# Moving a gated linear recurrent unit in front of the attention, with its input projections as seven-product tiles

## The reference, cut to what matters

```python
proj = h @ w_in                      # 1024 x 9216
q, k, v, g_att, u, g_lru, merge = jnp.split(proj, split_at, axis=-1)
y_a = (dilated_attention(q, k, v) * silu(g_att)) @ w_pa
u = causal_depthwise_conv(u, conv_w, conv_b)          # 4 taps
y_b = (rg_lru(u, ...) * silu(g_lru)) @ w_pb
gate_a, gate_b = jnp.split(sigmoid(merge), 2, axis=-1)
out = (gate_a * y_a + gate_b * y_b) @ w_o
```

## Time and profile before

| | |
|---|---|
| median of the timed runs | 2789.05 us |
| the profiled execution, its own time | 2786.48 us |
| its span | 2784.7 us |
| PE busy | 98% of the span |
| DVE, ACT, POOL busy | 72%, 56%, 11% |
| sets, from the first product to the last | 1753.67 to 2096.39 us |
| attention, up to the first tile of the recurrent unit | 2096.39 to 2344.88 us |

### The profile page before, as it was taken

One profiled execution on the slowest core, in us unless ns is written; L12 is line 12 of the kernel. 1 busy time (PEld: TensorE's weight loads), 2 busy tenths in 40 slices (PEclk: granted clock), 3 DMA queues, 4 the chain that ended last, 5 costly groups with the idle time before them and its releaser, 6 DMA issues.

```text
span 2784.7 us, 33128 instructions
## 1 busy us (share of the span) xinstructions
PE 2733.2 (98%) x13148; PEld 2280.7 (82%) x13148; DVE 2000.1 (72%) x2300; ACT 1558.0 (56%) x1724; POOL 301.9 (11%) x179
## 2 busy tenths in 40 slices
PE   8999999969999999999999998999999999999999
PEld 7888788858888888888888887888888888888887
DVE  7554457778888888888888888755555565666664
ACT  5322322247777777777777776322335666997122
POOL 0211000020000000000000001332321111112000
PEclk9999999989999999999999999999999999999999
DMA  6222248689999999999999964243333443114442
GB/s 198 95 75 65 87 153 291 247 344 375 385 385 386 387 386 386 386 384 390 384 386 384 386 228 164 95 121 111 101 121 134 129 122 102 49 48 144 169 149 91
DMA packets 181546, 628.30 MB, mean 226 GB/s; under 512 B 43920, under 2 KB 78096, under 8 KB 125840
## 3 DMA queue, kind: packets, MB, share of 16 engines
q1 hardware_dynamic: 176496, 609.46, 58.8%
q0 software_dynamic: 4464, 16.25, 2.2%
q10 hardware_dynamic: 432, 0.47, 0.1%
HBM read 557.74 MB, written 67.21 MB: 224 GB/s over the span
## 4 chain that ended last, share of the span: by engine, by line
PE 95%; DVE 3%; ACT 1%; DMA 1%; issue 0%; SPq 0%; DVEq 0%; ACTq 0%
PE bank L468 25%; PE bank L470 25%; PE bank L469 25%; PE bank L1894 13%; PE bank L476 3%; PE bank L2801 1%; PE bank L485 1%; PE bank L1443 1%; PE bank L794 1%; PE bank L3299 0%; DVE r_sc L1677 0%; DVE r_at L1678 0%; DVE r_best L1674 0%; PE bank L2802 0%; PE bank L854 0%
## 5 line engine op out<-in xcount | busy, mean ns | idle before, releaser
L1842 DVE TENSOR_TENSOR e_wl<-e_raw,e_wh 128x2048 fp32r<-128x2048 f32 x381 | 870.8, 2291 | 123.9 <-ACT e_wh L1834 123.5
L1834 ACT ACTIVATE e_wh<-e_raw 128x2048 fp32r<-128x2048 f32 x384 | 735.7, 1919 | 184.4 <-PE bank L470 101.0
L468 PE MATMUL bank<-e_wh,e_xh 128*128 128x512 f32 x1020 | 403.4, 395 | 0.0
L470 PE MATMUL bank<-e_wh,e_xl 128*128 128x512 f32 x1020 | 398.1, 390 | 0.0
L469 PE MATMUL bank<-e_wl,e_xh 128*128 128x512 f32 x1020 | 396.9, 389 | 0.0
L470 PEld LDWEIGHTS bank<-e_wh,e_xl 128*128 128x128 f32 x1020 | 191.4, 188 | 41.0
L469 PEld LDWEIGHTS bank<-e_wl,e_xh 128*128 128x128 f32 x1020 | 191.8, 188 | 38.1
L468 PEld LDWEIGHTS bank<-e_wh,e_xh 128*128 128x128 f32 x1020 | 191.6, 188 | 38.0 <-DVE e_wl L1842 0.4
L1894 PE MATMUL bank<-e_wh,e_hh 128*128 128x512 f32 x512 | 159.1, 392 | 0.0
L1894 PE MATMUL bank<-e_wl,e_hh 128*128 128x512 f32 x512 | 157.8, 389 | 0.0
L1894 PE MATMUL bank<-e_wh,e_hl 128*128 128x512 f32 x512 | 157.8, 389 | 0.0
(11 more groups left out here) (579 smaller groups left out, 5864.3 us busy)
## 6 DMA issues: line engine op xcount, KB each, us to landing
e_raw<-in_e_gate_dram SPq DMA_DIRECT2D x128, 1024.0 KB, 7.2
e_raw<-in_e_up_dram SPq DMA_DIRECT2D x128, 1024.0 KB, 7.5
e_raw<-in_e_down_dram SPq DMA_DIRECT2D x128, 1024.0 KB, 7.7
b_raw<-in_w_sets_dram SPq DMA_DIRECT2D x18, 1024.0 KB, 5.3
a_raw<-in_w_dram SPq DMA_DIRECT2D x12, 1024.0 KB, 5.7
a_mod_w<-in_w_mod_dram SPq DMA_DIRECT2D x48, 256.0 KB, 4.7
b_raw<-in_w_dram SPq DMA_DIRECT2D x11, 1024.0 KB, 4.9
a_x<-in_x_dram SPq DMA_DIRECT2D x16, 512.0 KB, 4.5
```

What stands on the lines that cost most here:

```text
L468: e.matmul(out, a[0], b[0], start=first, stop=False)
L470: return e.matmul(out, a[1], b[0], start=False, stop=last)
L1834: e.activation(t.e_wh[s][:, 0:2048], t.e_raw[slot][:, 0:2048], ACT.Copy).then_inc(*e.inc("e_round", i))
L1842: e.tensor_tensor(t.e_wl[s][:, 0:2048], t.e_raw[slot][:, 0:2048], t.e_wh[s][:, 0:2048].bitcast(F32), ALU.subtract).then_inc(*e.inc("e_spli ...
```

## The change

The recurrent unit is computed beside the sets. All 8 of its tiles become sets, at the front of the list; one merge tile takes the place of one of them in the half tiles of the attention, and 25 sets of seven products replace 18. The set loop calls one step of the unit after each product: the block of channels ct uses the products 9 + 21 ct and on, and `step` is the number of products since. The results of a set of the unit are stored to DRAM, and loaded again for the convolution and for the Silu. The place of `l_u`, `l_cv` is won by shortening the ring to 6 and AHEAD to 4, and one of the crossed blocks is put over a quarter of the input `h`, which is stored before and loaded again at the end of the sets. The unit's result goes to DRAM and comes back after the attention. The computation of `decay` (34 small DVE instructions) moves from the start of the attention to the first layer. POOL, which made the rests of the unit's rounded input and of its gates' weights before, still makes them, and takes over the last product (with Silu of the gate) from DVE.

```diff
-N_SETS = 18
+N_SETS = 25
-AHEAD = 6
-UNIT_TILE, MERGE_TILE = 1, 9
+AHEAD = 4
+N_RING = 6
+MERGE_TILE = 2
-HALF_SLOT = (3, 0, 1, 2, 3, 0, 1, 2, 3, 0, 1, 3, 0, 1)
+HALF_SLOT = (1, 3, 2, 0, 1, 3, 2, 0, 1, 3, 2, 1, 3, 2)
+SET_KINDS = ([("lru", i) for i in range(8)] + [("values", 2 + i) for i in range(4)]
+             + [("qk", 4 + i) for i in range(8)] + [("merge", i) for i in range(5)])
+LRU_FROM, LRU_EVERY, LRU_GATES = 9, 21, 6
+def lru_step(q):
+    ct, k = divmod(q - LRU_FROM, LRU_EVERY)
+    return (ct, k) if 0 <= ct < 8 else (-1, 0)
 def set_bank(g, i):
-    return (7 * g + i) % 8
+    q = 7 * g + i
+    return (q + 4 * gates_ahead(q)) % 8
 (pe_set, after product q)
+        if lru_step(q)[1] == LRU_GATES:
+            pe_lru_gates(e, t, lru_step(q)[0])
 (the loops of ACT and DVE over q; DVE's has dve_lru_step, SP's sp_lru_step)
         act_set(e, t, *divmod(q, 7))
+        act_lru_step(e, t, *lru_step(q))
+    e.wait_ge(*e.at("lru_made", 7))
 (act_lru_step: step 0 Identity for the first tap; 3 the two Copies that round;
  8 and 9 four Sigmoids each; 10 Exp, Tanh, Square; 12 Sqrt, Silu)
+    if step == 12:
+        e.wait_ge(*e.at("lru_q", ct))
+        e.activation(tt[:, :], tt[:, :], ACT.Sqrt, scale=-1.0, bias=t.k["tiny"])...
+        e.wait_ge(*e.at("l_gl_in", ct))
+        e.activation(t.l_u[:, :], t.l_u[:, :], ACT.Silu)...
 (dve_lru_step: step 0 two taps, 1 the third; 11 the two products; 13 product and scan)
 (pool_second)
     for g in range(1, N_SETS):
         pool_set_sums(e, t, g)
+        ct = (g - 2) // 3
+        if g % 3 == 2:
+            pool_lru_step(e, t, ct, 4)
+        if g % 3 == 1 and g > 1:
+            pool_lru_step(e, t, (g - 4) // 3, 14)
+    pool_lru_step(e, t, 7, 14)
 (sp_lru_step: step 2 loads the gate's input, 10 the next gates' weights, 15 stores
  the result when lru_made and loads the next block's u)
 (sp_second)
+    e.wait_ge(*e.at("b_hid", 1, 3))
+    for part in range(2):
+        e.dma_start(t.scr_b21[part], t.b_hid[part][:, 0:4, 512:1024].bitcast(F32))...
+            if q == 7 * (N_SETS - 1) + 3:
+                e.wait_ge(*e.at("part_spent", q))
+                (both parts of the quarter are loaded again)
 (dve_low_crossed and act_round_crossed: crossed block 2 waits until the early tiles are done)
+    if n == 2:
+        e.wait_ge(*e.at("w_spent", 1))
+        e.wait_ge(*e.at("hid_out1"))
 (dve_lru)
+    dve_low_w(e, t, MERGE_TILE)
     attention_over(e)
```

More of the change, by code:

```diff
@@ L1221, in dve_first @@
             dve_s5_inputs(e, t, b)
+        if slot == 12:
+            dve_decay(e, t)
         if slot % 8 == 6:
@@ L2127, in last_part_of @@
 def last_part_of(h):
-    return max(q for q in range(N_PARTS) if q % 8 // 2 == h)
+    return max(q for q in range(N_PARTS) if q % N_RING // 2 == h)
 def tile_slot(i):
-    return i if i < N_EARLY else (i - UNIT_TILE) % 2
+    return i % 2
 def sp_load_w(e, t, i):
@@ L2817, in unit @@
             which, half = u[1:]
-            pe_channels(e, t, unit_bank(u), wt, whole, t.b_hid, half, 8, ("lru_in", 0, which, half), behind=behind)
+            pe_channels(e, t, unit_bank(u), wt, whole, t.b_hid, half, 8, ("merge", 2 * which + half - 4), behind=behind)
         if unit_half_done(u):
@@ L3301, in pe_lru_gates, with act_lru_step @@
                     m.then_inc(*e.fill(b, "lru_gate", ct, half, k))
-def act_lru_gates(e, t, ct):
+def act_lru_step(e, t, ct, step):
     rt, it, at, tt = t.l_t
-    if ct:
-        e.wait_ge(*e.at("lru_made", ct - 1))
-    for half in range(2):
+    p = t.p
+    if ct < 0:
+        return
+    if step == 0:
+        e.wait_ge(*e.at("l_u_in", ct))
+        if ct:
+            e.wait_ge(*e.at("lru_iu", ct - 1))
+        e.activation(t.l_cv[:, :], t.l_u[:, :], ACT.Identity, scale=p["conv_w"][:, ct:ct + 1],
+                     bias=p["conv_b"][:, ct:ct + 1]).then_inc(*e.inc("conv_begun", ct))
+    if step == 3:
+        e.wait_ge(*e.at("conv_made", ct))
+        if ct:
+            e.wait_ge(*e.at("lru_made", ct - 1))
+        e.activation(t.l_cvs[0][:, :], t.l_cv[:, :], ACT.Copy).then_inc(*e.inc("cv_high", ct))
+        e.wait_ge(*e.at(f"l_wg_in{ct % 2}", ct))
+        e.activation(t.l_wgs[0][:, :], t.l_wg[ct % 2][:, :], ACT.Copy).then_inc(*e.inc("wg_high", ct))
+    if step in (8, 9):
+        half = step - 8
+        tok = slice(512 * half, 512 * half + 512)
+        if ct:
+            e.wait_ge(*e.at(f"lru_out{(ct - 1) % 2}", ct - 1))
@@ new lines, in act_lru_step @@
+    if step == 10:
+        e.wait_ge(*e.at("decay_made"))
+        then(e).activation(at[:, :], rt[:, :], ACT.Exp, scale=t.decay[:, ct:ct + 1]).then_inc(*e.inc("lru_a", ct))
+        e.wait_ge(*e.at("lru_a", ct))
+        e.activation(rt[:, :], rt[:, :], ACT.Tanh, scale=t.decay[:, ct:ct + 1]).then_inc(*e.inc("lru_th", ct))
+        e.activation(tt[:, :], at[:, :], ACT.Square).then_inc(*e.inc("lru_sq", ct))
+    if step == 12:
+        e.wait_ge(*e.at("lru_q", ct))
+        e.activation(tt[:, :], tt[:, :], ACT.Sqrt, scale=-1.0, bias=t.k["tiny"]).then_inc(*e.inc("lru_root", ct))
+        e.wait_ge(*e.at("l_gl_in", ct))
+        e.activation(t.l_u[:, :], t.l_u[:, :], ACT.Silu).then_inc(*e.inc("gl_made", ct))
@@ new lines, in sp_load_lru_gates, with lru_part_stored, sp_load_lru @@
+def sp_load_lru_gates(e, t, ct):
+    if ct < 8:
+        if ct >= 2:
+            e.wait_ge(*e.at("lru_parts", ct - 2))
+        e.dma_start(t.l_wg[ct % 2][:, :], t.ins["w_lru"][ct]).then_inc(*e.dma(f"l_wg_in{ct % 2}", ct))
+def lru_part_stored(e, ct, which):
+    for k, w, half in SET_OUT.values():
+        if w == which:
+            e.wait_ge(*e.at(f"set_out{2 * k + ct % 2}", ct))
+def sp_load_lru(e, t, ct):
+    if ct < 8:
+        lru_part_stored(e, ct, 0)
+        e.wait_ge(*(e.at("lru_made", ct - 1) if ct else e.at("w_spent", 1)))
+        e.dma_start(t.l_u[:, :], t.scr_lru_in[ct, 0]).then_inc(*e.dma("l_u_in", ct))
```

311 lines of the change are left out of this document (135 added, 176 removed).

## The result

The changed kernel takes 2811.1 us, the median of 2806.36, 2809.32, 2812.88 and 2812.89; the kernel before takes 2788.3 beside it. The ratio of the means is 1.0077, with a 95% interval of 1.0062 to 1.0093: slower by some 22 us (21.7 between the means, 22.8 between the medians). The profiled execution took 2806.36 us, 19.9 more than the one before.

A forecast was written before the change was run, and what follows sets the result against it. PE, busy 98% of the span, was taken to bound the kernel. 2786.48 - 19.9 + 0.5 + 43.9 (stalls) = 2811.0 us; with the median 2.6 us above the profiled execution, 2813.6 us. Range 2768 to 2834 us.

The forecast's parts named there:

- The matmuls removed: Seven tiles go from 96 to 84 matmuls, 19.0 us less; 0.86 us idle at the attention's end goes: together -19.9 us.
- The start of the sets: Crossed block 2 waits for the early tiles, delaying the feeds up to product 4: +0.5 us, bounds 0 and +3.
- The walk: One channel block's steps, timed from r, set 3's weights landing; product 27 (i = 6) 1.3 us late; all stalls 43.9 us.
- POOL beside the scan: DVE and POOL exclude one another; product, scan and rest each wait for a POOL sum, some 3.3 us in all.
- The chain through the load: Blocks chained through SP's weight load: period 62.6 us against PE's 58.9, 3.7 us stall each; first six blocks 2.2 + 18.5.
- The merge sets: Block 6: ACT's sigmoids wait for DVE's additions, unit steps queue behind, 15.1 us; block 7, without sums beside its scan, 5.0.
- The end: End of the sets: first half tile's rest behind POOL's last product, +2.1 us; late reload of the stored quarter, +1.0.
- The drain at table loads: Skill's 1.38 us drain per ACT table switch would add 5.5 us per block, about 2858 us in sum; left out.
- Rival 3, the clock: Stalls lower PE's clock to half: 19 us more, 2833 us if all eight do, 2821 with three; chance 0.19.
- rival 1: All the unit's work beside the sets stays hidden: 2769 us; chance 0.18.
- rival 2: One late product per block, no chain: 8 x 1.3 = 10 us lost, 2779 us; chance 0.14.
- rival 4: The gain is eaten exactly, by about 20 us of stalls and a chain period near 60 us: 2789 us; chance 0.07.

The follow-up runs named there:

- The last version: Changed kernel with earlier load, later Silu, later merge-set sigmoids, three orders outside the blocks, and the quarter's reload issued before the last set's stores: 2771.94 us, ratio 0.9941.
- the earlier load and the later Silu: Changed kernel with both SP's earlier load of set weights and ACT's Silu one step later, behind product 26's rounding: 2786.50 us, ratio 0.9995.
- the earlier load alone: Changed kernel, but SP loads set g + 2's weights in step 3 of set g, not step 0 of set g + 1: 2795.11 us, ratio 1.0020.
- the kernel with tiny sums: Changed kernel, but POOL's sums of sets 4, 7, ... 22 are made on one column only: 2786.87 us, ratio 0.9995.
- both edits and the sigmoids: Changed kernel with earlier load, later Silu, and the merge sets' sigmoids two products later: 2775.75 us, ratio 0.9960.
- the kernel in which POOL waits for the scan: Changed kernel, but POOL waits for the unit's scan before the sums of sets 4, 7, ... 22: 2815.81 us, ratio 1.0098.
- scan later: Changed kernel, but DVE makes the unit's product and scan one step later, behind the rest of product 27: 2810.43 us, ratio 1.0074.

## Why the prediction was right, point by point

The forecast of 2813.6 us stands against 2811.1. The stated range, 2768 to 2834 us, also held cases in which the change wins, so being inside it says little; the likeliest case, 2800 to 2826, is what came. Its mechanism, blocks chained through SP's load, is shown by the runs. Several sizes were off, and one agreement is luck.

- **The matmuls removed (-19.0, and -0.9 of idle time).** The last version has nearly no stalls and is at 2771.9. Take away its two waits and what resuming costs, some 3 us, and it is within 1 or 2 us of 2787.8 - 19.9. The gap of the earlier trace rows did go, but a wait of 1.5 us for a sigmoid took its place; this the prediction had waved through.
- **The start of the sets (+0.5).** PE has no idle time there. 0.
- **The walk.** Measured from r = 1925.03, in brackets as predicted: Silu ends at 19.9 (19.9), product 26 is rounded at 20.4 (20.5), the rest of 27 is done at about 28.6 (29.1), the last addition at 37.4 (38.4), the next landing at 43.7 (44.5). So the steps hold within a microsecond. The steps of the next set are a little shorter too, and r comes again after 61.1 us (62.6); the other distances of r are 60.4, 62.5, 63.0 and 61.0.
- **POOL beside the scan.** Right in kind, too large in size: product and scan take 1.82 + 3.26 us instead of 1.22 + 2.29, and from the end of the addition ahead of them to the end of the rest of 27 it is 6.8 us, where 7.4 were predicted. The sign "scans at 3.5 us and more" was not met. Nor is the lock enough by itself: with the earlier load and the later Silu the scan is still 3.27 us and PE waits for nothing in the six blocks.
- **The chain through the load.** Right and the largest single part: the earlier load alone gives back 16 us. The period was sized at 62.6 and is 61.7, so the block's loss is 2.7 us and not 3.7. From the first product of the sets to product 27 of block 5 it is 2139.17 - 1753.25 = 385.92 us; the kernel with tiny sums, which stalls nowhere till then, takes 2123.44 - 1753.48 = 369.96. The loss is 16.0 us; 20.7 were predicted. The prediction called itself wrong in the chain if PE's waits were near 1 us: three of the six are 2.1 us and more, the others 0.6 or none. It is the period and the run with the earlier load that speak for the chain, not the size of the waits.
- **The merge sets (15.1 and 5.0).** The whole of the sets takes 2279.48 - 1753.25 = 526.23 us, and 175 products and eight gates need 175 x 2.72 + 8 x 1.82 = 490.56 (the last version takes 491.61). That is 35.7 us lost, 19.7 of them after product 27 of block 5, where 20.1 were predicted (the steps named for block 6 give 9.1 + 67.5 - 62.1 = 14.5, not quite its 15.1). The cause is the one named, ACT standing at a sigmoid: without it all but 0.72 us of the waits are gone. The closeness of the number is luck: PE waits there for 12.4 us only, and the other 7.3 us are half clock and resuming, which the sum had no term for.
- **The end (3.1).** Half right. POOL's rest of the half tile was not late (0 instead of 2.1); the reload was, by 1.9 instead of 1.0. The part after the sets takes 524.7 us, where the kernel before would give 688.3 - 7 x 21.76 - 8 x 1.82 - 0.86 = 520.5: 4.2 us lost, the reload's 1.9, the sigmoid's 1.5 and 0.8 that no single row shows.
- **The drain at table loads.** A load of 1.28 us stands at 1925.68 and the next ACTIVATE at 1926.98, as in the earlier trace rows. The Trainium skill (ScalarE: Activation LUTs, What ACT_TABLE_LOAD costs) adds a drain of 1.38 us at every switch. No row here shows it, and the prediction's estimate by it, 2858 us, would have been 47 us too high.
- **Rival 3, the clock.** Partly true, and it did not make the kernel slower than forecast. The clock fell after six of the stalls. Of the 35.7 us lost in the sets PE's waits are 21.7 (18.3 + 3.4); the other 14.0 are half clock and resuming. In the first six blocks most of what PE loses at half clock it does not have to wait for at the next product 27, since DVE, ACT and SP set the period. But not all of it: in the block after each fall ACT stands waiting for PE's product 21, by 1.15, 0.45 and 0.50 us. The first of them:

```profile
1878.13 0.60 ACT L2489 ACTIVATE b_sy<-bank 128x512 f32<-128x512 f32 x1 [1.15 <-PE bank L472]
```

So in the six blocks the rival's sum counts most of the clock's cost twice, and a sum without any clock counts it too low. No run has the clock apart, and for the merge sets the rows don't tell.
- **Rivals 1, 2 and 4** are out by the time, and rivals 1 and 2 each have a kernel: the load alone is nearly rival 2 (0.6 us late per block, no chain, 2795 with the merge sets' stalls), both edits and the sigmoids rival 1.

The total came out closer than its terms. Against the kernel before the profiled spans give: start of the sets -0.4 us (1753.25 instead of 1753.67; +0.5 predicted), first six blocks 16.0 (20.7), merge sets 19.7 (20.1), end 4.2 (3.1). That is 39.5 us where 44.4 were predicted, and the profiled execution is 4.6 us below the predicted 2811.0 (its own time is 2.2 us over its span, 1.8 before). The step that was mis-sized is the chain's period, by 0.9 us a block.

## What to carry to other kernels

When work is put beside a stage that one engine bounds, follow one full round of the feeding engines until the same event comes again, with the transfers in it: if that period is longer than the bound engine's, every round stalls, whatever slack the first had. Look in that round for a wait that is longer than its reason, here a load queued behind a store that it does not need; moving one DMA issue was worth 16 us, moving the unit's last product from POOL to DVE nothing. Time that the bound engine loses inside such a round is mostly, though not wholly, time for which it would have waited; so a lower clock there must not simply be added to the waits.

## What the runs showed that was not expected

PE's clock fell to half, 1.2 GHz, in the products after stalls of only 1.8 to 2.1 us, and near 1.8 us it went both ways. Stretches of 8 us of the kernel in which POOL waits for the scan, after idle times of 1.81, 1.80, 1.77 and 1.78 us:

```profile
1861.00:1869.00 8.00, 7.65 (x39) 6.06 (x40) 3.07 (x6) 0.74 (x2) 1.00 (x2) 1.00 0.72 231
1923.00:1931.00 8.00, 7.30 (x30) 5.53 (x31) 3.33 (x6) 0.35 (x1) 0.95 (x2) 0.79 0.70 231
1986.00:1994.00 8.00, 7.45 (x38) 5.91 (x39) 3.18 (x6) 0.07 (x1) 0.52 (x2) 1.00 0.88 235
2050.00:2058.00 8.00, 7.96 (x33) 6.03 (x34) 3.10 (x6) 1.07 (x2) 1.05 (x1) 0.79 0.76 229
```

Two stay at full clock, two do not. The fall also comes late: in the changed kernel, after the stall of 2.12 us, PE starts a matmul each 0.23 us at first, and from 1832.32 on, 1.5 us after it resumed, each 0.43. After 1.47, 1.63 and 1.90 us (scan later) the clock stayed at 1.00, after 1.87, 2.11, 2.55 and 2.65 it was 0.79 in the 8 us behind. The idle time alone does not decide: at the start of the attention PE waited 2.81 us for the reload (the version with the later sigmoids) and 2.87 us (POOL waits), and the clock stayed at 1.00 both times.

```profile
2256.00:2264.00 8.00, 7.31 (x32) 6.10 (x33) 0.00 (x0) 0.00 (x0) 0.00 (x0) 1.00 0.78 291
```
